# A depthwise convolution with four taps on the rows and four channel groups on column tiles of TensorE

## The reference

```python
def conformer_conv(u, conv_w, conv_b, ln_g, ln_b):
    a, b = jnp.split(u, 2, axis=-1)
    h = a * jax.nn.sigmoid(b)                                         # GLU
    C = h.shape[-1]                                                   # 1024
    h = lax.conv_general_dilated(h, conv_w[:, None, :].astype(h.dtype), (1,), [(CONV_KERNEL - 1, 0)],
                                 dimension_numbers=('NWC', 'WIO', 'NWC'), feature_group_count=C) + conv_b
    return jax.nn.silu(layer_norm(h, ln_g, ln_b))
```

## Time and profile before

| | before |
|---|---|
| median of 3 runs | 2020.38 (2019.88 to 2021.5) |
| the profiled execution | 2024.76 |
| its span, on the slowest core (7) | 2023.5 |
| spans of the other cores | 2007.9 to 2014.6 |
| convolution's matmuls in that profile | 647.4 to 766.9 |
| mean granted clock of core 7 | 0.954 of full speed |

### The profile page before, as it was taken

The page is one execution under the profiler, slowest core; times in us unless marked ns, Lnnn a source line. Parts: engine busy times, 40 slices in busy tenths (PEclk is TensorE's granted clock), DMA queues, the critical chain, the costliest instruction groups (busy, mean ns, idle before and its releaser), DMA issues.

```text
span 2023.5 us, 30136 instructions; the slowest of 8 cores (2007.9 to 2023.5 us)
## 1 busy us (share of the span) xinstructions
PE 1820.6 (90%) x10944; PEld 995.8 (49%) x10944; DVE 825.8 (41%) x1571; ACT 519.6 (26%) x912; POOL 126.5 (6%) x129
## 2 busy tenths in 40 slices
PE   3799998989977992997775999999999999999999
PEld 2466546666643441886333444444444444444444
DVE  3344124556555684224366143241441423414224
ACT  3233245777765134102324000000000000000000
POOL 1100100000000000100000000100001001010000
PEclk9899999999988996998796999999999999999999
DMA  9721965422422001984112353917628357184454
GB/s 209 141 84 42 116 72 75 69 54 33 74 54 32 0 1 53 235 108 63 21 22 42 42 75 51 126 29 97 88 38 125 46 80 102 23 125 58 68 84 166
DMA packets 187536, 153.12 MB, mean 76 GB/s; under 512 B 13312, under 2 KB 176768, under 8 KB 183040
## 3 DMA queue, kind: packets, MB, share of 16 engines
q0 software_dynamic: 173968, 107.13, 39.9%
q1 hardware_dynamic: 13424, 44.07, 6.5%
HBM read 249.78 MB, written 8.52 MB: 128 GB/s over the span
## 4 chain that ended last, share of the span: by engine, by line
PE 81%; DMA 5%; DVE 5%; another core or an unknown queue 4%; ACT 2%; issue 2%; POOL 1%; SPq 0%; DVEq 0%; ACTq 0%; POOLq 0%
PE pair L1250 15%; PE bank L1252 15%; PE pair L1267 8%; PE bank L1267 8%; PE pair L521 4%; PE bank L521 4%; DMA arena<-sel 4%; PE pair L1052 3%; PE pair L1123 3%; PE bank L1123 3%; PE bank L1052 3%; PE pair L803 2%; PE bank L782 2%; PE bank L676 2%
## 5 line engine op out<-in xcount | busy, mean ns | idle before, releaser
L1250 PE MATMUL pair<-arena 128*128 128x512 bf16 x1408 | 319.8, 380 | 0.0
L1252 PE MATMUL bank<-arena 128*128 128x512 bf16 x1408 | 318.2, 379 | 0.0
L1255 DVE TENSOR_TENSOR arena<-bank,arena 128x512 bf16<-128x512 f32 x88 | 60.9, 692 | 548.5 <-PE pair L1250 449.5
L1254 ACT ACTIVATE arena<-pair 128x512 bf16<-128x512 f32 x88 | 52.5, 597 | 823.9 <-PE pair L1250 804.2
L792 ACT ACTIVATE arena<-bank,arena 128x512 bf16<-128x512 f32 (+3 forms) x402 | 215.1, 574 | 75.4 <-PE pair L803 31.0
L1250 PEld LDWEIGHTS pair<-arena 128*128 128x128 bf16 x1408 | 138.2, 98 | 167.0 <-issue 2.1
L1252 PEld LDWEIGHTS bank<-arena 128*128 128x128 bf16 x1408 | 137.7, 98 | 166.2
L1267 PE MATMUL pair<-arena 128*128 128x512 bf16 x704 | 168.1, 379 | 0.0
L1267 PE MATMUL bank<-arena 128*128 128x512 bf16 x704 | 166.3, 379 | 0.0
L469 PE MATMUL bank<-arena 128*128 128x128 bf16 x544 | 53.2, 276 | 113.8 <-DVE arena L461 113.8
L803 PE MATMUL pair<-arena 128*128 128x129 bf16 (+1 forms) x1184 | 124.8, 226 | 20.2 <-DVE arena L796 18.0
(11 more groups left out here) (174 smaller groups left out, 1853.0 us busy)
## 6 DMA issues: line engine op xcount, KB each, us to landing
arena<-xc SPq DMA_DIRECT2D x24, 1024.0 KB, 9.5
arena<-w_gate POOLq DMA_DIRECT2D x22, 1024.0 KB, 11.2
arena<-w_up POOLq DMA_DIRECT2D x22, 1024.0 KB, 12.8
arena<-w_down POOLq DMA_DIRECT2D x22, 1024.0 KB, 11.2
arena<-w_in POOLq DMA_DIRECT2D x18, 1024.0 KB, 13.6
arena<-w_out POOLq DMA_DIRECT2D x8, 1024.0 KB, 31.3
y<-arena SPq DMA_DIRECT2D x8, 1024.0 KB, 3.9
arena<-sel SPq DMA_DIRECT2D x28, 256.0 KB, 4.1
```

Of the source, the lines that this page charges most:

```text
L1250: op(PE, lambda: nc.tensor.matmul(bank[pg][:, :], lhsT=wgt[:, kc, cc * 128:(cc + 1) * 128], rhs=h3T[:, kc, tc * 512:(tc + 1) * 512], start ...
L1252: op(PE, lambda: nc.tensor.matmul(bank[pu][:, :], lhsT=wut[:, kc, cc * 128:(cc + 1) * 128], rhs=h3T[:, kc, tc * 512:(tc + 1) * 512], start ...
```

## The change

A round now takes one half's 512 positions of 128 channels as four groups of 32 channels. For each group a copy of its GLU output is laid out with 4 taps on the partitions: partition 32 i + c of tile `h4` holds channel c shifted by i positions. One matmul of 128 rows by 32 columns so sums 4 taps of 32 channels, and 8 steps make 32 taps, the first with weight zero. The four groups of a step write partitions 32 g to 32 g + 31 of one bank: each is on its own 32 columns of the array. A round has 32 matmuls of 512 positions in place of 31.

The tiles `h4` come from `hglu` by four DMAs on SP each (32 partitions, 4 channel groups, 540 positions). There are seven tiles. The first seven rounds' are loaded at the end of `u_proj`, where the projection's input tile is now given up to make room; the others in the convolution, when the round that used the tile has been emitted. The diagonal weights are 128 x 32 x 32 elements instead of 128 x 31 x 128, built on POOL, the first two at the end of `u_proj`, the others two rounds ahead. On the host the channels are reordered, in the convolution's parameters and in the rows of `w_out`, to the order in which the rounds now produce them; a small constant (four 32 x 32 identities) is added.

```diff
-        cid = self.tile(G, "cid", [128, 256], BF16)
+        cid = self.tile(G, "cid", [128, 288], BF16)
...
         def u_proj():
...
                 wrel()
+            P1.close()
+            self.free(hTb + [htailb])
+            for j in range(NH4):
+                h4.append(self.tile(HG, f"h4_{j}", [128, 4, 544], BF16))
+                h4b.append(self.buf(f"h4_{j}"))
+            for j in range(2):
+                dg.append(self.tile(HG, f"dg{j}", [128, 32, 32], BF16))
+                dgb.append(self.buf(f"dg{j}"))
+            for k in range(NH4):
+                h4_load(k)
+            for k in range(2):
+                build_dg(k)
+
+        NH4 = 7
+        h4, h4b, dg, dgb = [], [], [], []
+        id4 = cid[:, 256:288].unsqueeze(1).broadcast_to([128, 32, 32])
+
+        def h4_load(k):
+            tc, half, qd = k // 8, (k % 8) // 4, k % 4
+            j = k % NH4
+            for i in range(4):
+                c0 = tc * 512 + 1 + i
+                dma(SP, h4[j][32 * i:32 * i + 32, :, 0:540], hglu[32 * qd:32 * qd + 32, 4 * half:4 * half + 4, c0:c0 + 540], r=hglub[4 * half:4 * half + 4], w=[h4b[j]] if i == 0 else [], pw=[] if i == 0 else [h4b[j]], owner=h4b[j])
+
+        def build_dg(k):
+            ch_ = k % 8
+            wv = pvec[:, PV_CW + ch_ * 32:PV_CW + ch_ * 32 + 32].unsqueeze(2).broadcast_to([128, 32, 32])
+            op(POOL, lambda: nc.gpsimd.tensor_tensor(out=dg[k % 2][:, :, :], in0=id4, in1=wv, op=ALU.mult), r=[cidb, pvb], w=[dgb[k % 2]])
...
-        P1.close()
-        self.free(hTb + [htailb])
         A.close()
...
-        dg = [self.tile(CV, f"dg{j}", [128, 31, 128], BF16) for j in range(2)]
...
-        def build_dg(n):
-            ch_ = n % 8
-            wv = pvec[:, PV_CW + ch_ * 31:PV_CW + ch_ * 31 + 31].unsqueeze(2).broadcast_to([128, 31, 128])
-            op(DVE, lambda: nc.vector.tensor_tensor(out=dg[n % 2][:, :, :], in0=ident_b, in1=wv, op=ALU.mult), r=[cidb, pvb], w=[dgb[n % 2]])
-
         it_ = 0
-        build_dg(0)
         for tc in range(2):
             for ch in range(8):
-                dj = it_ % 2
-                if it_ + 1 < 16:
-                    build_dg(it_ + 1)
+                psi = rot_proj.next()
+                hj, dj = it_ % NH4, it_ % 2
+                for st in range(8):
+                    for g in range(4):
+                        op(PE, lambda: nc.tensor.matmul(bank[psi][32 * g:32 * g + 32, :], lhsT=dg[dj][:, 8 * g + st, :], rhs=h4[hj][:, g, 4 * st:4 * st + 512], start=(st == 0), stop=(st == 7), skip_group_check=True), r=[dgb[dj], h4b[hj]], w=[bankb[psi]])
+                if it_ + NH4 < 16:
+                    h4_load(it_ + NH4)
+                if it_ + 2 < 16:
+                    build_dg(it_ + 2)
                 it_ += 1
-                psi = rot_proj.next()
-                for j in range(31):
-                    o = 2 + j + tc * 512
-                    op(PE, lambda: nc.tensor.matmul(bank[psi][:, :], lhsT=dg[dj][:, j, :], rhs=hglu[:, ch, o:o + 512], start=(j == 0), stop=(j == 30)), r=[dgb[dj], hglub[ch]], w=[bankb[psi]])
...
+CPERM = np.arange(1024).reshape(2, 4, 4, 32).transpose(0, 2, 1, 3).reshape(1024)
...
+    cw = f(I["conv_w"])[0][:, CPERM]
+    taps = np.concatenate([np.zeros((1, 1024), np.float32), cw], axis=0)
+    pv[:, PV_CW:PV_CW + 256] = taps.reshape(8, 4, 32, 32).transpose(1, 3, 2, 0).reshape(128, 256)
```

## The result

The changed kernel takes 1968.24 us (median of 4 runs, 1966.37 to 1968.34) against 2020.94 (4 runs, 2019.88 to 2023.56): 0.9735 of the time before, interval 0.9718 to 0.9752, faster by 52.7. Forecast were 1953.6 and, as range with the two rivals that save less, 1946 to 1980; the forecast's own range was 1947 to 1965. The profiled execution took 1968.34, of a span of 1966.9 on core 1; the one before took 2024.76, on core 7. On both cores the last GLU write begins at 576.6 (in the earlier trace rows for before), so positions in the two traces can be laid side by side.

The account below looks back on a forecast made before the run. PE streaming past diagonal weights, 7.13 a round, bounds the convolution; start at 642.8, rounds of 2.7, turn 5.8, then rounds of 3.66 bring the last bias pass 66.8 earlier: 1958.0 profiled, 1953.6 median; range 1947 to 1965 (60%).

Parts of the forecast that it names:

- the two rivals that save less: POOL and DVE blocking each other (15%, time 1974) and copies reloaded too late in the convolution (10%, time 1977).
- 1.73 a round: PE streaming in the convolution: four column groups side by side cost 8 x 0.216 = 1.73; one after another 6.91.
- the slower rival: Convolution on PE: groups run one after another with weight loads unhidden, a round 10.7, +52, time 2072; chance 9%.
- The turn: Between the convolution's halves: square's end to exponential's end takes 5.8 as before, putting bias pass 8 at 673.2.
- ACT's loop of 3.66: Convolution's second half: with a Silu each round, bias passes on ACT follow 3.66 apart, which binds that half.
- The copies: Tile loads on SP, 4.5 a tile: first 28 DMAs behind the selection maps, 595.3 to 627; later ones in time.
- The step that failed: Start of the convolution: builds 0 and 1 run on POOL in the attention's tail, PE starts at 642.8, not 647.43.
- PE waiting for ACT alone in the second half: Sign named for the forecast being right: in the convolution's second half PE waits for nothing but ACT.
- The rival that came true in mechanism: POOL's builds and DVE's casts block each other in the convolution: 15.6 + 4.8 less saved, time 1974; chance 15%.
- Build time: One 1024-element diagonal build on POOL: bounds 0.96 and 3.8, 2.67 estimated, taken as 2.7 with its hop; binds first half.
- The clock: PE's clock in the second half, idling 1.3 a round: costed at nothing; at the lower level seven rounds cost 6.6.
- The offset: Profiled execution of before, 2024.76, stood 4.4 above the median of 2020.38; so forecast 1958.0 became 1953.6.

## Why the prediction was right and wrong

**The direction and the bulk were right.** Columns side by side gave 1.73 a round as taken, not the 2.9 that the prediction estimates from the ratio of the Trainium skill ("TensorE: Matmul & The Clock Gate", Part 3); the weight loads stayed hidden, so the slower rival falls. The Trainium skill ("TensorE: Matmul & The Clock Gate", Part 3) says that a load overlaps matmuls in flight only where row groups differ; here all groups share all rows, and 32 loads and matmuls in 1.73 disagree. The turn, forecast at 5.8 from the end of the square to the end of the exponential, kept its length: bias passes 7 and 8 are 8.1 apart where 7.8 was forecast. ACT's loop of 3.66 measured 3.48 where nothing disturbed it. The copies were hidden, in the order forecast, behind the selection maps. Yet the time lies outside the forecast's own range, 1947 to 1965, and inside 1946 to 1980 only by the rivals in it.

**The step that failed** is that PE starts at 642.8, "when the last transposes are through": builds 0 and 1 moved into the attention's tail, were costed on POOL's own queue alone (behind the mask products and two `w_out` loads), and the tail was left as long as before. There DVE's products with the maps were stretched (0.23 to 0.43 became 2.0 to 2.2), which PE waits for: 3.5 on the profiled core, 6.3 by the medians. The two differ because 642.8 was read on core 7 of before, whose own tail of 65.8 is 3.2 above the median. The same omission stands in the second half's loop of 3.66, read "with nothing else on DVE" and kept with builds beside it: 4.4. The step named the queue that the builds stand in and left out what they share with the engine PE was waiting for. The sign "PE waiting for ACT alone in the second half" came true and could not show this: ACT in turn was waiting for stretched instructions of DVE.

**The rival that came true in mechanism** had 15%: POOL and DVE block each other. Its size was off. It priced the second half at 15.6, the cast of each of six builds held for all of 2.6; in the trace five DVE instructions lost 5.76, since a build is shorter and its beginning drifts against the round. Against ACT's real loop of 3.48 instead of 3.66, what shows is 4.4. The tail it did not price at all. Its time of 1974 was nearer to 1968.24 than the forecast's.

**The reading that misled** is the earlier trace rows: three DVE products in 1.36 within 2.0 beside four POOL products of 1.87, taken as proof that they don't exclude each other. The two rows merge instructions of different sizes. One by one, in the trace of before, they show the opposite: POOL's products begun ahead of DVE's take 0.42, the two behind them 0.60 and 0.54, and DVE's product of 384 elements beside them takes 0.47, where the twelve away from POOL's products take 0.35 to 0.36.

```profile
525.58 0.42 POOL L876 TENSOR_TENSOR arena<-arena 128x128 bf16<-128x128 bf16 x1
525.97 0.60 POOL L876 TENSOR_TENSOR arena<-arena 128x128 bf16<-128x128 bf16 x1
...
526.31 0.47 DVE L796 TENSOR_TENSOR arena<-arena 128x384 bf16<-128x384 bf16 x1
...
535.62 0.36 DVE L796 TENSOR_TENSOR arena<-arena 128x384 bf16<-128x384 bf16 x1
```

, 415/478/667, holds both kinds, and the prediction took its median for a product by itself. So the trace did not disagree with the rival; it showed it in small, and the rows of a short instruction were carried to one eight times as long.

**Build time.** Taken at 2.67 from the bounds 0.96 and 3.8, measured 1.91: more of a short product is its start than the memsets suggested. From 0.416 for 128 elements and 1.91 for 1024 come 0.20 to start and 1.67 ns an element (an estimate), where the prediction has 0.09 and 2.5. It made the first half's bound look right by accident: rounds came 2.80 apart against 2.7, yet not by POOL's throughput but by the chain bias pass, stretched cast, square, statistics on PE; with the builds on DVE they are 2.4 apart.

**The clock** stood at 0.82 in the second half, PE idling between rounds. Costed at nothing, it cost nothing that shows: the undisturbed rounds ran at ACT's pace.

**The offset** of 4.4 between profiled execution and median was carried over as if fixed. It depends on which core is slowest in that execution, and after the change it was 0.1.

## What to carry to other kernels

Before moving work to an idle engine, ask what it shares with the busy ones, not only whether its queue is free: here 1.9 us of reading on POOL cost DVE up to 2.0 each time, and the same work on DVE, 1.2 and built once for both halves, took 0.8% of the kernel's time less (0.9656 against 0.9735). When a row is used to exclude contention, take it apart into single instructions, compare each with its like elsewhere in the trace, and let it be of the length of the instruction it stands for. And when a stage shrinks to half, list the limits in order: here PE's streaming, POOL and DVE, ACT's chain at 3.5, the copies, and each appeared when the one before it was taken away.

## What the runs showed that was not expected

Four column groups ran side by side at a quarter of the time that they need one after another, 1.73 for 32 matmuls, weight loads included. By the recorded starts, PE starts matmuls out of program order past ones whose columns are taken: blocks of four on a group keep full pace (1.78), blocks of eight don't (4.4). And a POOL memset of the same size, 0.95, leaves DVE's two-input products alone where a POOL product of 1.91 stops them, and is itself held up by DVE.
